# Gathering the experts' rows from the fp32 state by scaled placements instead of from three bf16 parts

## What is computed

```python
def moe(h, router_w, router_b, w_gate_up, b_gate_up, w_down, b_down):
    logits = (xt @ router_w + router_b).astype(jnp.float32)
    top_val, top_idx = lax.top_k(logits, TOP_K)
    gates = jax.nn.softmax(top_val, axis=-1).astype(h.dtype)
    ...
        gu = xb @ w_gate_up[e] + b_gate_up[e]
        g, u = gu[:, :D_FF], gu[:, D_FF:]
        g = jnp.minimum(g, SWIGLU_LIMIT)
        u = jnp.clip(u, -SWIGLU_LIMIT, SWIGLU_LIMIT)
        act = (u + 1) * (g * jax.nn.sigmoid(SWIGLU_ALPHA * g))
        return (act @ w_down[e] + b_down[e]) * wb[:, None]
    ...
h = h + moe(rms_norm(h, ffn_norm_w[l]), ...)
```

## Time and profile before

| | us |
|---|---|
| median of 3 runs | 1114.68 (1114.57 to 1117.3) |
| the profiled execution, its time | 1115.29 |
| its span | 1113.7 |
| TensorE busy | 1052.6 (95% of the span) |
| VectorE busy | 283.6 (25%) |
| ScalarE busy | 156.5 (14%) |
| DMA | 432.88 MB, 389 GB/s over the span |

### The profile page before, as it was taken

How to read it: one execution, slowest core, us unless ns; L and a number is a source line. 1 busy time by engine, 2 the same in 40 slices (tenths; PEclk the granted TensorE clock), 3 DMA queues, 4 the chain that set the end, 5 groups by cost and what they waited for, 6 DMA issues and landing times.

```text
span 1113.7 us, 14686 instructions
## 1 busy us (share of the span) xinstructions
PE 1052.6 (95%) x6239; PEld 486.9 (44%) x6239; DVE 283.6 (25%) x718; ACT 156.5 (14%) x321; POOL 30.2 (3%) x32
## 2 busy tenths in 40 slices
PE   9999999999999999979999989889898997999997
PEld 7788875543333333333343333333333342333333
DVE  2698862651111111111111111111010121111111
ACT  3453341410000000000000000000000010000011
POOL 1000071000000000000000000000000000000000
PEclk9999999999999999999999989999999998999999
DMA  9933298799999999999999999999999999999996
GB/s 286 357 97 114 76 351 343 292 409 434 431 431 441 430 428 433 432 432 433 433 433 433 439 440 424 443 415 444 428 435 431 424 443 423 429 431 430 425 426 270
DMA packets 42287, 432.88 MB, mean 389 GB/s; under 512 B 3827, under 2 KB 22590, under 8 KB 28206
## 3 DMA queue, kind: packets, MB, share of 16 engines
q1 hardware_dynamic: 41934, 432.30, 92.9%
q0 software_dynamic: 160, 0.04, 0.1%
q10 hardware_dynamic: 160, 0.07, 0.0%
HBM read 431.35 MB, written 1.05 MB: 388 GB/s over the span
## 4 chain that ended last, share of the span: by engine, by line
PE 65%; DMA 32%; ACT 1%; issue 1%; DVE 0%; SPq 0%; ACTq 0%
DMA arena<-in_w_gate_up 31%; PE psum L1002 27%; PE psum L1039 13%; PE psum L795 5%; PE psum L675 3%; PE psum L968 3%; PE psum L848 3%; PE psum L875 2%; PE psum L1049 2%; PE psum L1019 1%; PE psum L975 1%; DMA arena<-in_x 1%; PE psum L1024 1%; ACT arena L1418 1%; PE psum L786 1%
## 5 line engine op out<-in xcount | busy, mean ns | idle before, releaser
L1002 PE MATMUL psum<-arena 128*64 128x512 f32 x2048 | 461.8, 609 | 39.5 <-DMA arena<-in_w_gate_up 30.9
L1002 PEld LDWEIGHTS psum<-arena 128*64 128x64 f32 x2048 | 154.1, 140 | 341.0 <-issue 314.7
L1039 PE MATMUL psum<-arena 128*64 128x512 f32 x992 | 218.3, 592 | 0.0
L1754 DVE TENSOR_SCALAR arena<-psum 128x512 f32<-128x512 f32 x32 | 22.1, 692 | 723.0 <-PE psum L1002 718.4
L1039 PEld LDWEIGHTS psum<-arena 128*64 128x64 f32 x992 | 69.4, 137 | 127.8 <-issue 124.6
L1405 ACT COPY arena<-psum 128x256 f32<-128x256 f32 x32 | 11.9, 373 | 554.0 <-PE psum L975 554.0
L1049 PE MATMUL psum<-arena 64*128 64x512 f32 x248 | 61.6, 614 | 6.8 <-ACT arena L1418 6.8
L795 PE MATMUL psum<-arena 128*128 128x256 f32 x256 | 59.0, 380 | 0.3 <-ACT arena L1300 0.3
L1418 ACT COPY arena<-psum 128x512 f32<-128x512 f32 x31 | 18.2, 587 | 238.4 <-PE psum L1039 238.4
L795 PEld LDWEIGHTS psum<-arena 128*128 128x128 f32 x256 | 47.7, 190 | 8.0 <-issue 1.2
L968 PE MATMUL psum<-arena 128*128 128x64 bf16 x1488 | 48.8, 191 | 2.2
(11 more groups left out here) (252 smaller groups left out, 580.3 us busy)
## 6 DMA issues: line engine op xcount, KB each, us to landing
arena<-in_w_down SPq DMA_DIRECT2D x26, 4096.0 KB, 31.0
arena<-in_w_gate_up SPq DMA_DIRECT2D x20, 4096.0 KB, 32.9
arena<-in_w_gate_up SPq DMA_DIRECT2D x18, 2048.0 KB, 18.4
arena<-in_w_down SPq DMA_DIRECT2D x8, 2048.0 KB, 25.7
arena<-in_w_gate_up SPq DMA_DIRECT2D x11, 1024.0 KB, 9.5
arena<-in_w_in SPq DMA_DIRECT2D x9, 1024.0 KB, 6.9
arena<-in_w_down SPq DMA_DIRECT2D x6, 1024.0 KB, 9.8
arena<-in_w_in SPq DMA_DIRECT2D x8, 512.0 KB, 8.6
```

Of the source, the lines that this page charges most:

```text
L1002: last = mm(b[64 * half:64 * half + 64, :], xe[i][:, k, :], channels(slot_gu[slot][:, j, o:o + FF], half), start=(k == 0 and first), stop= ...
L1039: last = mm(b[64 * c:64 * c + 64, :], aT[:, j, 64 * h:64 * h + 64], slot_dn[slot][:, j, c * 512:(c + 1) * 512], start=False, stop=(h == DC ...
```

## The change

- `gather` takes fp32 operands: the stationary one is `h1_row(t, k)`, 128 words of the state with seven between each two, the moving one the placement. It has 8 steps x 2 halves of the tokens, 16 calls.
- The placement `ph` is fp32 and holds the token's scale `rsh` in place of the 1 (`build_rows`).
- The split is gone from ScalarE and VectorE, with its semaphores and the wait of the first `gather`.
- `h1` stays whole during all experts. `ph` and `g_s`, `aT`, `a_s`, `y_s` lie where `hT`, `mixT` and `xn3` lay.
- Beside it, two semaphores of the attention part (`ckv_ready`, `kpe_ready`) become one (`latent_ready`) that counts to 2; who waits for what is the same. That part of the diff is left out below.

```diff
-        ph = [half_words(at), half_words(WB + 5120), half_words(at + 64)]; at += 128
+        ph = [grid(WB + 2048 + 2 * SLOTS * i, 2, SLOTS) for i in range(3)]
...
-        xn3 = words(WB, 3072).bitcast(BF16).rearrange("p (t s d) -> p t s d", t=2, s=3)
-        remains = xe[0].rearrange("p k s -> p (k s)").rearrange("p (b n) -> p b n", b=2)
-        at = WB + 3072
+        at = WB
         g_s = words(at, 512); at += 512
         aT = grid(at, 4, P); at += 512
...
-        def h1_rows(t, c):
+        def h1_row(t, k):
 
-            return h1[:, t, :].rearrange("p (q j) -> p j q", j=KD)[:, c * GR:(c + 1) * GR, :]
+            return h1[:, t, :].rearrange("p (q j) -> p j q", j=KD)[:, k, :]
...
                 for k in range(KD):
                     for t in range(2):
-                        for part in range(3):
-                            last = mm(X[:, k * SLOTS:(k + 1) * SLOTS], xn3[:, t, part, k * P:(k + 1) * P],
-                                      ph[i][:, t, :], start=(t == 0 and part == 0), stop=(t == 1 and part == 2))
+                        last = mm(X[:, k * SLOTS:(k + 1) * SLOTS], h1_row(t, k), ph[i][:, t, :], start=(t == 0),
+                                  stop=(t == 1))
                 last.then_inc(S.gathered, 1)
...
-            pe.wait_ge(S.split_ready, 2 * GC)
             gather(1, SIDE[0])
...
-            act.wait_ge(S.logits_ready, 2)
-            high_part(0)
-            high_part(1)
-            for m in range(2 * GC):
-                middle_part(m)
-                if m + 2 < 2 * GC:
-                    high_part(m + 2)
...
-                return ts(ph[i][:, t, :], columns(base), rankp[:, t, col], None, ALU.is_equal)
+                return ts(ph[i][:, t, :], columns(base), rankp[:, t, col], rsh[:, t:t + 1], ALU.is_equal, ALU.mult)
...
-            remains_of(0)
-            for m in range(2 * GC):
-                if m + 1 < 2 * GC:
-                    remains_of(m + 1)
-                low_part(m)
```

More of the change, by code:

```diff
@@ L109, in bank_plan @@
     add("ckv", 6, "squares", 1)
-    add("kpe", 7, "kpe_ready", 1)
+    add("kpe", 7, "latent_ready", 2)
     add("par", 5, "par_ready", 1)
@@ L308, in layer @@
         tk = words(at, 512); at += 512
-        def half_words(at):
-            return words(at, 64).bitcast(BF16).rearrange("p (t s) -> p t s", t=2)
         wp = [grid(at, 2, P), grid(WB + 5248, 2, P), grid(at + 256, 2, P)]; at += 512
-        ph = [half_words(at), half_words(WB + 5120), half_words(at + 64)]; at += 128
+        ph = [grid(WB + 2048 + 2 * SLOTS * i, 2, SLOTS) for i in range(3)]
         pick = [words(at + 32 * i, 32).bitcast(BF16) for i in range(ROUND - 1)] + [words(WB + 5184, 32).bitcast(BF16)]; at += 128
@@ L372, in layer @@
         in_early = {k: sem(f"in_early{k}") for k in list(EARLY) + ALONE}
-        for name in ("cols_clear pads_clear zero_clear pa_ready par_ready meta_ready xss_ready xroot_ready root_turned raw_ready raw_act diag_ready rs_ready hn_ready ckv_ready "
-                     "squares kpe_ready lvar_ready lroot_ready lat_ready csig_ready convin_ready v_ready "
+        for name in ("cols_clear pads_clear zero_clear pa_ready par_ready meta_ready xss_ready xroot_ready root_turned raw_ready raw_act diag_ready rs_ready hn_ready "
+                     "squares latent_ready lvar_ready lroot_ready lat_ready csig_ready convin_ready v_ready "
                      "kraw_ready qraw_ready ksq_ready qsq_ready khvar_ready khroot_ready qhvar_ready qhroot_ready k_ready q_ready "
@@ L379, in layer @@
                      "router_ready logits_ready bound_ready exp_done mask_ready rank_ready place_ready "
-                     "hi_ready remains_ready mid_ready split_ready cnt_ready gate_ready overflow_ready bias_step used built gathered "
+                     "cnt_ready gate_ready overflow_ready bias_step used built gathered "
                      "part_used xe_half xe_ready turned sT_ready g_ready a_step sg_ready act_ready aT_done aT_ready y_ready scattered0 scattered "
@@ L400, in layer @@
                     for i, name in enumerate(pieces)}
-        piece_used = {"kv": (S.kpe_ready, 1), "q": (S.squares, 2)}
+        piece_used = {"kv": (S.latent_ready, 2), "q": (S.squares, 2)}
         piece_used.update({("c", j): (S.csig_ready, j + 1) for j in range(CT)})
@@ L747, in _ @@
                                              stop=True))
-            pe.wait_ge(S.kpe_ready, 1)
+            pe.wait_ge(S.latent_ready, 2)
             b = fill("kpet")
@@ L1243, in _ @@
             scales_out(1)
-            act.wait_ge(S.ckv_ready, 1)
+            act.wait_ge(S.latent_ready, 1)
             f(sqk, ckvn, ACT.Square).then_inc(S.squares, 1)
@@ L1512, in _ @@
             scaled(1)
-            tt(ckvn, full("ckv")[:, 0:L], rs_row, ALU.mult).then_inc(S.ckv_ready, 1)
-            tt(kpeT, full("kpe")[:, 0:L], rs_row, ALU.mult).then_inc(S.kpe_ready, 1)
+            tt(ckvn, full("ckv")[:, 0:L], rs_row, ALU.mult).then_inc(S.latent_ready, 1)
+            tt(kpeT, full("kpe")[:, 0:L], rs_row, ALU.mult).then_inc(S.latent_ready, 1)
             dve.wait_ge(S.par_ready, 1)
@@ L1541, in _ @@
             conv_in(0)
-            dve.wait_ge(S.kpe_ready, 1)
+            dve.wait_ge(S.latent_ready, 2)
             ts(rsb, full("ssk")[:, 0:L], 1.0 / KVL, EPS, ALU.mult, ALU.add).then_inc(S.lvar_ready, 1)
```

## The result

The changed kernel takes 1305.52 us (1302.56 to 1308.87, 4 runs) beside 1115.74 us of the kernel before; the ratio is 1.169 (95% interval 1.167 to 1.172). It is slower, as forecast, but by 190 us instead of 125, and 40 us above the range. The profiled execution has a span of 1301.7 us.

The account below looks back on a forecast made before the run. The prediction took the weights' DMA as slower than TensorE before, and TensorE alone as the bound after. 1059.5 us without waits plus 31 x 5.8 us gave 1239, plus 1.6 outside the span, rounded to 1240 us; range 1120 to 1265.

Parts of the forecast that it names:

- TensorE's and the weights' pace: In the expert loop before the change: TensorE 26.26 us per expert, the weights' DMA 29.1 us.
- the split hidden: Removing the split on ScalarE and VectorE, hidden under the first expert's matmuls, gains 0.
- The number of pairs: In the fp32 gather: 16 calls become 32 load-and-multiply pairs, 992 in the changed profile.
- all waits for weights go: In the expert loop: TensorE at 32.1 us per expert, above the weights' 29.1, no longer waits for them.
- The price of a pair: In the gather: 0.23 us per strided load-and-multiply pair, so 7.4 us a gather, 5.8 more than before.
- the 1.8 ns of the split's operation: VectorE's time per strided word in the split, used to price a 128-word load at 0.23 us.
- The doubling of TensorE's own loads: Transpose loads 16 bytes apart take about double; doubling the ordinary 0.112 us a pair gives 0.224.
- The sum without the clock: Whole kernel: 1059.5 us without weight waits plus 31 gathers x 5.8 us, together 1239.
- a rival at 0.12: Sparse gather drops TensorE's clock to 1.2 GHz, adding 30 times 2.2 us: 1306 us; chance 0.12.
- Its sign: What would show the clock rival in the profile: long matmuls behind the gather at more than 14 us.
- The rival of a free stride: Gather pairs take 0.112 to 0.12 us, 2.0 to 2.3 us more per gather: 1124 to 1132 us; chance 0.27.
- An edit that costs TensorE up to 1.7 us per expert could at best be hidden: In the expert loop: TensorE's 53.0 us lost to weight waits and slower clock, over 31 experts, taken as reserve.

Follow-up runs that it names:

- the ordered copy: Changed kernel plus one fp32 copy of the state in the weights' order, half each on ScalarE and VectorE, so gather weights are neighbouring words; 1134.29 us, ratio 1.015.
- the two experiments with 64 and 32 columns a pair: Changed kernel with neighbouring words as gather weights: each call made twice (64 columns), 1275.42 us; each call split into two of 32 columns, 1414.57 us.
- the run with neighbouring words: Changed kernel with neighbouring words of the state as the gather's weights, the rows' channel order left out; 1133.33 us, ratio 1.014.

## Why the prediction was wrong, step by step

- **TensorE's and the weights' pace, and the split hidden**: right. The split's 16 operations are gone, VectorE idles before its first clamp for 7.81 us instead of 4.61, and the second gather starts at 226.41 us, as before.
- **The number of pairs** (992) and that all waits for weights go: right.
- **The price of a pair**, forecast 0.23 us: measured (7.70 - 0.335) / 31 = 0.238 for the loads, 0.245 with what stands around them, a gather of 7.86 us instead of 7.4. The term was sized almost right: 31 x 0.46 = 14 us short, which would still have been inside the range. One of its two reasons stood on thin ground, though: the ordered copy read the same strided words on VectorE in 1.10 us for 1024, 1.07 ns each, so the 1.8 ns of the split's operation was not the price of the stride on VectorE alone. The doubling of TensorE's own loads was the sound argument.
- **The sum without the clock**: 1059.5 + 31 x 6.3 = 1255 us of span. The measured 1301.7 has 47 us more, 31 times 1.5. Every one of the 31 gathers loses the clock.
- **The step that failed** is the clock: the prediction put its loss at nothing in the sum, had it as a rival at 0.12 and left it out of the range. Its words against it, that the records leave no idle time between the gather's matmuls, were wrong as a reason: the records show matmuls in flight, not columns streaming, and the two experiments with 64 and 32 columns a pair show that the columns matter. The rival's price of 2.2 us per expert was too high (1.5) and, with the cheaper pair, landed on 1306 us; the match is in part luck. Its sign, the long matmuls behind the gather at more than 14 us, named the wrong ones: the gate and up matmuls still take 13.95 us, and the second projection, nearer to the gather, pays.
- **The rival of a free stride** would have come out at 1133 us (1131 to 1136), as the run with neighbouring words shows, at or just above the upper end of its 1124 to 1132.
- **"An edit that costs TensorE up to 1.7 us per expert could at best be hidden"**: too generous. The total of the waits is not all reserve, because the first 8 MB load needs its slots early; 1.33 us per expert already cost 4.7 us there, and 7.5 us in all.

## What to carry to other kernels

Count what the array streams, not only whether TensorE is busy: a row of short matmuls behind slow weight loads keeps "busy" at 100% and can still lose the clock, and then the next, dense stage pays. Lay a stationary fp32 operand so that at least two of its words share 16 bytes, or its load takes twice as long; where the load was hidden before, the matmul becomes as long as the load. And a sum of waits over a whole loop hides only a part of what is added: look for the one transfer that needs its buffers earliest, and for how close the loop's code is to being fetched anew each turn.

## What the runs showed of the hardware

- Ordinary fp32 weight loads of 128 columns: 0.112 to 0.117 us a pair with words one apart, 0.125 with two, 0.24 with four or eight, 0.22 with sixteen, at 64 streamed columns. The strided ones keep this pace at a granted clock of 1.00 and of 0.50 alike (10 pairs in 2.00 us, 11 in 2.30); those of neighbouring words, with 32 columns streamed, went from 0.11 us a pair at 1.00 to 0.22 at 0.50.
- The granted clock fell to 0.50 in a gather with 64 columns per 0.245 us and in one with 32 columns per 0.11 us, and held in one with 64 columns per 0.115 us. Cutting the first kind into stretches of 4.0 us did not keep it. A stream of gather and projection in turns, two calls and four matmuls, held it at 1.00 in 29 experts and left it at 0.50 for some 25 us in one.
- Copying 1024 words of the state from 32 bytes apart took ScalarE 2.04 us and VectorE 1.10 us.
- A loop of five experts whose TensorE code is some 40 loads and matmuls longer than the kernel before was stopped for 4.7 to 6.6 us at the start of each turn, with 18 packets on the instruction queue in two turns, where the kernel before had none.
